# A gated recurrence whose decays are products raised in place instead of exponentials of sums, in a float32 forward pass on one core

## The reference, cut to what matters

```python
def hg_gate(z, lb):                       # lb is 0 in the first block
    k = (1.0 - lb) * sigmoid(-z)
    log_f = log(lb + (1.0 - lb) * sigmoid(z))
    return k, log_f
# S_t = diag(f_t) S_{t-1} + k_t v_t^T,  o_t = S_t^T q_t, by chunks:
    cum = cumsum(lf)
    s_new = exp(last)[..., None] * s + einsum('bhsd,bhse->bhde', kc * exp(last - cum), vc)
    o_inter = einsum('bhtd,bhde->bhte', qc * exp(cum), s)
    decay = exp(where(mask, cum[t] - cum[s], -inf))
    att = einsum('bhtd,bhsd,bhtsd->bhts', qc, kc, decay)
    o = o_inter + einsum('bhts,bhse->bhte', att, vc)
```

## Time and profile before

| | |
|---|---|
| runs | 4153.04, 4154.2, 4158.31 us |
| profiled execution | 4154.1 us, span 4152.8 us, clock 0.941 |
| busy in the span | PE 3831.2 us (92%), DVE 1727.9 (42%), ACT 1230.5 (30%), POOL 216.7 (5%) |
| recurrence, first block | from 437.6 to 592.05 us |
| recurrence, second block | from 1536.2 to 1653.88 us |

### The profile page before, as it was taken

How to read it: one execution, slowest core, us unless ns; L and a number is a source line. 1 busy time by engine, 2 the same in 40 slices (tenths; PEclk the granted TensorE clock), 3 DMA queues, 4 the chain that set the end, 5 groups by cost and what they waited for, 6 DMA issues and landing times.

```text
span 4152.8 us, 46787 instructions
## 1 busy us (share of the span) xinstructions
PE 3831.2 (92%) x20116; PEld 3083.9 (74%) x20116; DVE 1727.9 (42%) x2151; ACT 1230.5 (30%) x1582; POOL 216.7 (5%) x162
## 2 busy tenths in 40 slices
PE   7989678999998876999989989889998999998997
PEld 5866577888887556788868867568886887676886
DVE  3135764222233267433443346543335334354334
ACT  3125432211122263322232234432223223333222
POOL 0000320000000014000000002000000000000000
PEclk9989779999998996999999999899999999999998
DMA  6415101111121100222312222012222222221222
GB/s 247 149 58 188 50 18 47 68 61 61 61 72 61 67 6 1 81 102 93 109 68 95 101 92 81 21 70 92 102 95 78 91 102 101 71 91 62 101 94 79
DMA packets 47709, 341.74 MB, mean 82 GB/s; under 512 B 5280, under 2 KB 5440, under 8 KB 7696
## 3 DMA queue, kind: packets, MB, share of 16 engines
q1 hardware_dynamic: 41184, 301.09, 20.3%
q0 software_dynamic: 5280, 35.57, 2.3%
q10 hardware_dynamic: 1040, 2.10, 0.1%
HBM read 336.63 MB, written 2.10 MB: 82 GB/s over the span
## 4 chain that ended last, share of the span: by engine, by line
PE 86%; DVE 9%; ACT 3%; issue 1%; POOL 1%; DMA 1%; DVEq 0%; ACTq 0%; POOLq 0%
PE PS L349 66%; PE PS L351 7%; PE PS L815 2%; DVE SQ L443 2%; PE PS L831 1%; PE PS L1386 1%; PE PS L870 1%; PE PS L390 1%; PE PS L1112 1%; DVE nmax_a L965 1%; DVE YS L1829 1%; PE PS L409 1%; DVE att L1579 1%; PE PS L502 1%; DVE X L1836 1%
## 5 line engine op out<-in xcount | busy, mean ns | idle before, releaser
L326 DVE TENSOR_TENSOR WL<-raw,WH 128x2048 fp32r<-128x2048 f32 x260 | 595.9, 2292 | 414.9 <-ACT WH L321 414.9
L321 ACT ACTIVATE WH<-raw 128x2048 fp32r<-128x2048 f32 x260 | 495.4, 1905 | 464.5 <-PE PS L349 346.6
L349 PE MATMUL PS<-XH_ff,WH 128*128 128x512 f32 x704 | 280.4, 398 | 12.1 <-DVE XL_ff L454 12.1
L349 PE MATMUL PS<-XH_b,WH 128*128 128x512 f32 x704 | 276.9, 393 | 11.9 <-DVE XL_b L454 10.5
L349 PE MATMUL PS<-XH_a,WH 128*128 128x512 f32 x704 | 277.1, 394 | 11.4 <-DVE XL_a L454 10.0
L349 PE MATMUL PS<-XH_ff,WL 128*128 128x512 f32 x704 | 280.2, 398 | 0.0
L349 PE MATMUL PS<-XL_ff,WH 128*128 128x512 f32 x704 | 277.7, 394 | 0.0
L349 PE MATMUL PS<-XL_a,WH 128*128 128x512 f32 x704 | 275.5, 391 | 0.0
L349 PE MATMUL PS<-XH_a,WL 128*128 128x512 f32 x704 | 275.3, 391 | 0.0
L349 PE MATMUL PS<-XL_b,WH 128*128 128x512 f32 x704 | 275.2, 391 | 0.0
L349 PE MATMUL PS<-XH_b,WL 128*128 128x512 f32 x704 | 275.0, 391 | 0.0
(11 more groups left out here) (356 smaller groups left out, 7815.5 us busy)
## 6 DMA issues: line engine op xcount, KB each, us to landing
raw<-in_panels SPq DMA_DIRECT2D x260, 1024.0 KB, 4.8
ada_at<-in_ada_panels SPq DMA_DIRECT2D x24, 1024.0 KB, 4.8
ada_win<-in_ada_panels POOLq DMA_DIRECT2D x18, 1024.0 KB, 5.1
ada_start<-in_ada_panels POOLq DMA_DIRECT2D x6, 1024.0 KB, 22.5
FX<-in_dft_x POOLq DMA_DIRECT2D x2, 2048.0 KB, 8.0
X<-in_xT SPq DMA_DIRECT2D x1, 3072.0 KB, 11.2
out<-X ACTq DMA_DIRECT2D x1, 2048.0 KB, 6.9
rope<-in_rope POOLq DMA_DIRECT2D x2, 768.0 KB, 10.0
```

What stands on the lines that cost most here:

```text
L321: H.up(ac.activation(WH[s].rearrange("p k n -> p (k n)"), raw[:, s, :], ACT.Copy), n)
L326: L.up(ve.tensor_tensor(WL[s].rearrange("p k n -> p (k n)"), raw[:, s, :], WH[s].bitcast(F32).rearrange("p k n -> p (k n)"), ALU.subtract), n)
L349: t = te.matmul(PS[:, j, :], lhsT, x[:, k, 0:SEQ], start=st, stop=end)
```

## The change

The decays are products of gates rather than exponentials of sums. `tot[d][2h]` holds the product of the gates of each block of 2h tokens, made by multiplying the two halves of `tot[d][h]`. The units run from h = 1 to 64, with the directions alternating (`level_of`). QP (queries times gates) and the keys in U are raised in place: after unit u, the queries of the later halves are multiplied by the product of their earlier half, and the keys of the earlier halves by the product of their later half, which makes them ready for unit u + 2 of the same direction. DVE raises the queries (in the first block those of one of the two feature tiles; POOL those of the other), POOL raises the keys of all 768 tokens. After the last unit QP and the keys are what `state_outputs` and `turn_keys` need. `diffs`, `exps`, the scan, the logarithms, `starts` and the factors on POOL go away.

There is one `att` for both directions. Units 12 and 13 (h = 64) multiply only the 64 early keys and are copied by ACT without a mask. The self products (key sum times query) move to POOL and their matmul behind unit 5; increments and states of both directions come after the last unit; the mask arrives as bytes. Cut to its core:

```diff
-        b["cum"] = shelf.take(f"cum_{l}", [P, 2, 2, TOK])
-        b["ring"] = [shelf.take(f"ring{s}_{l}", [P, 2, TOK]) for s in range(3)]
-        b["att"] = [shelf.take(f"att{d}_{l}", [P, 2, 2 * (NT if l == 0 else NX), P]) for d in range(2)]
+        for k in ("F", "QP"):
+            b[k] = [shelf.take(f"{k}{d}_{l}", [P, 2, TOK]) for d in range(2)]
+        b["KQ"] = shelf.take(f"KQ_{l}", [P, 2, TOK])
+        b["att"] = shelf.take(f"att_{l}", [P, 2, 2 * (NT if l == 0 else NX), P])
+        b["tot"] = [{h: shelf.take(f"tot{d}{h}_{l}", [P, 2, TOK // h]) for h in (2 << i for i in range(LEVELS))}
+                    for d in range(2)]
...
         def level_of(u):
-            return u // LEVELS, u % LEVELS, P >> (u % LEVELS + 1)
+            return u % 2, 1 << (u // 2)
+        def level_bank(u, g, hh):
+            return 4 * (u % 2) + 2 * g + hh
+        def self_bank(l, fc):
+            return 2 * fc if l == 0 else 2 + fc
+        def own_features(l, g):
+            if l == 0:
+                return slice(1, 2) if g else slice(0, 1)
+            return None if g else slice(0, 2)
+        def raise_queries(eng, l, u, f):
+            q = halves(b["QP"][d][:, f, 0:N], h)[:, :, :, late]
+            by = totals(l, d, h)[:, f, 0:N // h].rearrange("p f (b t) -> p f b t", t=2)[:, :, :, d:d + 1]
+            return eng.tensor_tensor(q, q, by.broadcast_to([P, f.stop - f.start, N // (2 * h), h]), ALU.mult)
+        def raise_keys(eng, l, u):
+            k = halves(mix1[l]["U"][:, UFF + 2 * d:UFF + 2 * d + 2, :], h)[:, :, :, early]
+            by = totals(l, d, h).rearrange("p f (b t) -> p f b t", t=2)[:, :, :, 1 - d:2 - d]
+            return eng.tensor_tensor(k, k, by.broadcast_to([P, 2, TOK // (2 * h), h]), ALU.mult)
 # gp_hgrn
+            G.up(gp.tensor_tensor(b["KQ"][:, :, 0:N], U[:, UFF:UFF + 2, 0:N], U[:, UFB:UFB + 2, 0:N], ALU.add))
+            gp.wait_ge(*G.now())
+            G.up(gp.tensor_tensor(b["KQ"][:, :, 0:N], b["KQ"][:, :, 0:N], U[:, UHQ:UHQ + 2, 0:N], ALU.mult),
+                 (name, "kq"))
             for u in range(UNITS):
-                gp.wait_ge(*A[(name, "exp", u)])
-                gp.tensor_tensor(ww[:, :, :, late], ww[:, :, :, late], qq[:, :, :, late], ALU.mult)
-                G.up(gp.tensor_tensor(ww[:, :, :, early], ww[:, :, :, early], kk[:, :, :, early], ALU.mult), ...)
+                gp.wait_ge(*T[(name, "level", u, len(hgrn_groups(l)) - 1)])
+                if u >= 2:
+                    gp.wait_ge(*V[(name, "tot", level_of(u))])
+                    gp.wait_ge(*G[(name, "raised", u - 2)])
+                t = raise_keys(gp, l, u)
+                f = own_features(l, 1)
+                if f:
+                    t = raise_queries(gp, l, u, f)
+                G.up(t, (name, "raised", u))
 # te_hgrn: level(u), after the waits for QP and keys, or for raised u - 2 of G and V
+                            keys = early if h == HD else slice(0, P)
+                            t = te.matmul(PS[keys, to, x * HD:(x + 1) * HD],
+                                          U[r, UFF + 2 * d + f, j * P + keys.start:j * P + keys.stop],
+                                          queries[:, :, late], start=True, stop=True)
+            for g in range(3):
+                turn_values(g)
+            for u in range(UNITS):
+                level(u)
+                if u == 5:
+                    self_products(0)
+                    self_products(1)
+            for d in range(2):
+                turn_keys(d)
+                increments(d)
+            outputs()
+            for d in range(2):
+                state_outputs(d)
 # ac_hgrn, in this order: sigmoids, values, silu, units 12 and 13, turned keys
+                A.up(ac.activation(b["F"][d][:], z, ACT.Sigmoid), (name, "sg", d))
+                A.up(ac.activation(z, z, ACT.Sigmoid, scale=-1.0), (name, "sk", d))
+                A.up(ac.activation(b["hVT"][:, 2 * g:2 * g + 2, :], ...ACT.Copy), (name, "v", g))
+            for u in (UNITS - 2, UNITS - 1):
+                        ac.wait_ge(*V[(name, "pred", UNITS - 3, g, hh)])
+                        A.up(ac.activation(b["att"][early, hh, 2 * c0:2 * c1, late], PS[early, ...], ACT.Copy), ...)
 # ve_hgrn
-                    V.up(ve.tensor_scalar(f, f, 2.0 ** -63, None, ALU.max), (name, "f", d, fc))
+                V.up(ve.tensor_tensor(b["QP"][d][:, :, 0:N], U[:, UHQ:UHQ + 2, 0:N], F[:, :, 0:N], ALU.mult),
+                     (name, "QP", d))
+            for h in (2 ** i for i in range(LEVELS)):
+                for d in range(2):
+                    V.up(ve.tensor_tensor(b["tot"][d][2 * h][:].unsqueeze(3), parts[:, :, :, 0:1], parts[:, :, :, 1:2],
+                                          ALU.mult), (name, "tot", (d, 2 * h)))
+            for u in range(UNITS):
+                raised(u)
+                if u < UNITS - 2:
+                    preds(u)
+                if u == 5:
+                    self_terms(0)
+                    self_terms(1)
+            for d in range(2):
+                states(d)
```

More of the change, by code:

```diff
@@ L1370, in increments, with into @@
[L1370 to L1378, removed]
+                for to in increment_banks(d):
+                    bank(to, V, name, "S", d)
+            opened = set()
+            def into(j, f, hh):
+                to = 4 + 2 * f + j // 4
+                first = (to, hh) not in opened
+                opened.add((to, hh))
+                return PS[hh * HD:(hh + 1) * HD, to, (j % 4) * P:(j % 4 + 1) * P], first
@@ L1379, in level, with outputs @@
+            def outputs():
+                te.wait_ge(*V[(name, "preds")])
+                te.wait_ge(*A[(name, "preds")])
+                for to in range(4, 8):
                     wait_bank(to)
-                    wait_bank(to + 1)
-                    for x in range(2 * (c1 - c0)):
-                        j, f = c0 + x // 2, x % 2
+                for j in range(N // P):
+                    for f in range(2):
                         for hh in range(2):
[L1384 to L1405, removed]
+                            to, first = into(j, f, hh)
@@ L1406, in outputs, with state_outputs @@
+                            te.matmul(to, b["hVT"][:, j, f * P + hh * HD:f * P + (hh + 1) * HD],
+                                      b["att"][:, hh, 2 * j + f, :], start=first, stop=False, skip_group_check=True)
+            def state_outputs(d):
+                te.wait_ge(*V[(name, "S", d)])
+                te.wait_ge(*V[(name, "raised", UNITS - 2 + d)])
                 for j in range(N // P):
-                    i = order.index(j)
+                    i = visits(d).index(j)
                     for f in range(2):
@@ L1445, in ac_hgrn @@
             fence(ac, f"at{l}")
-            for fc in range(2):
-                A.up(ac.activation(U[:, UG + fc, 0:N], U[:, UG + fc, 0:N], ACT.Silu), (name, "g", fc))
             if l:
@@ L1462, in ac_hgrn @@
-            for d in range(2):
-                ac.wait_ge(*V[(name, "end", d)])
-                edge = P - 1 if d == 0 else 0
-                A.up(ac.activation(b["el"][d][:], b["cum"][:, d, :, edge::P], ACT.Exp), (name, "el", d))
-                A.up(ac.activation(b["ring"][d][:], b["ring"][d][:], ACT.Exp), (name, "end", d))
-            def keys(d):
-                if d:
-                    ac.wait_ge(*T[(name, "inc", 0)])
+                z = U[:, UFF + 2 * d:UFF + 2 * d + 2, :]
+                A.up(ac.activation(b["F"][d][:], z, ACT.Sigmoid), (name, "sg", d))
@@ new lines, in ac_hgrn @@
+            for u in (UNITS - 2, UNITS - 1):
+                late, early = sides(*level_of(u))
+                for g, (c0, c1) in enumerate(hgrn_groups(l)):
+                    ac.wait_ge(*T[(name, "level", u, g)])
+                    for hh in range(2):
+                        ac.wait_ge(*V[(name, "pred", UNITS - 3, g, hh)])
+                        A.up(ac.activation(b["att"][early, hh, 2 * c0:2 * c1, late],
+                                           PS[early, level_bank(u, g, hh), 0:2 * (c1 - c0) * HD].rearrange(
+                                               "p (c t) -> p c t", t=HD), ACT.Copy),
+                             (name, "pred", u, g, hh), (name, "preds"))
@@ L1482, in starts @@
-            def starts(d):
-                cu = b["cum"][:, d, :, 0:N]
-                A.up(ac.activation(cu, cu, ACT.Exp), (name, "start", d))
-            keys(0)
-            exps(0)
-            keys(1)
-            for u in range(1, UNITS):
-                exps(u)
-                if u % LEVELS == LEVELS - 1:
-                    starts(u // LEVELS)
             for fc in range(2):
```

280 lines of the change are left out of this document (116 added, 164 removed).

## The result

The changed kernel took 4059.2 us (median of 4 runs, 4054.4 to 4074.3) against 4156.3 for the kernel before beside it: ratio 0.977, 95% interval 0.9741 to 0.9799. Two later series of it gave 0.9815 (0.9789 to 0.9842) and 0.9794 (0.9769 to 0.9819). Forecast were 4097 us and 57 us less; by their ratios the three series say 96, 77 and 86 us less.

What follows compares the result with a forecast made beforehand. DVE bounds the first block's units, PE close behind; afterwards PE bounds. Savings of 35 us in the first block and 22 in the second, together 57 off 4154.1, give 4097 us; range 4076 to 4117.

Steps and rivals of the forecast that it cites:

- Prologue: Ahead of unit 0, log, scan, distances and factors go: unit 0 at 446.3 us instead of 479.25 in the first block.
- The start of the units: Unit 2 waits for DVE's 14 block products and first raise: stall 3.4 us (0 to 6) in the first block.
- Units at 1.2 GHz: Recurrence units in the lower clock: PE bounds at 5.39 us (first block) and 3.6 (second), plus stalls of 2 and 4.
- the rival that had it wait each time: DVE or turn-taking bounds the units: every DVE raise waits for POOL's keys; 4114 us, chance 0.16.
- The clock: Each block has one 9 us stretch of higher clock behind the self products, at 3.5 us a unit (2.5 in the second).
- the bare end: Behind the last unit: turned keys and increments 11.5 us, pairs 2.84, states about 6, no longer hidden in the first block.
- The prediction's own sign of being wrong: Wrong if POOL's products exceed 5 us a unit, PEclk stands at 1.00 in units, or DVE, not PE, never idles there.
- The first rival: Higher clock for all units: some 16 us less in the first block, 9 in the second; 4072 us, chance 0.12.
- h = 64: Units 12 and 13 load only 64 keys: 2.7 us for 48 matmuls and 1.8 for 32, or no gain (5.39).
- POOL's repeated operand: POOL's key raises in the units, never shown with a repeated operand, at plain price; up to twice as upper end.
- The slower rival: POOL's products with a repeated operand far slower: 2.7 times plain price spends the gain, three times gives 4170 us; chance 0.04.

Runs made afterwards that it cites:

- spread products: Changed kernel with DVE's block products spread two by two behind the first units' masked copies, not all ahead of the first raise: 4068.5 us, 0.9789 to the kernel before.
- late self products: Changed kernel with the self products behind unit 11 instead of unit 5: 4091.5 us, ratio 0.9852 to the kernel before.

## Why the prediction was wrong

The range began at 4076 us; the direction and the mechanism were right, the size was not.

- **Prologue.** Right. Unit 0 stood 8.8 us behind ACT's first table load in the first block (449.17 less 440.41), 8.8 forecast; in the second 8.9, forecast 9.1.
- **The start of the units.** Stalls of 7.8 and 10.0 us instead of 3.4 and 4.5. DVE's turns with POOL were foreseen at the upper end (457) and were worse, DVE was through at 464.4: two products took 8.31 us and the rest as long again, because each POOL operation (3.4 and 4.0 us, then 2.9, 1.5, 2.2 and 1.3) held a DVE product until it had ended. That cost 4 and 5 us against the forecast, and the spread products show that it was this queue.
- **Units at 1.2 GHz.** 20.75 us for units 2 to 5 instead of 23.6, 14.0 instead of 18.4 in the second block: the stalls for DVE (2 and 4 us) did not come. DVE starts its raise 0.05 us ahead of POOL's keys and so pays no turn; the rival that had it wait each time failed here, and came true in the kernel with spread products.
- **The clock. This is the step that failed.** "I give each block one such stretch of 9 us": in the first it lasted from 492 to past 530 us. Units 6 to 13 took 21.5 us instead of 33.5, and the bare end 15 instead of 20.5, since it too ran at 2.4 GHz. That is 12 + 5 us of the first block's 16 beyond the forecast (51 against 35; the rest of the terms cancel). In the second block the forecast's 9 us were near (7 us in two profiles, none in the third), and only the end was faster, 13.3 us instead of 18. The prediction's own sign of being wrong, PEclk at 1.00 in the units, came true from unit 6 on. The 9 us came from a stretch of the kernel before which ended at 496.6 us, when PE had just stood idle for 3.2; I took it for the length that such a stretch has, and let it only be shorter in the range. The same trace has a second fast stretch, of 13.7 us (547.8 to 561.4), that also ended behind a wait. PE behind the two waits (kernel before):

```profile
496.18 5.07 PE L1386 MATMUL PS<-ring 64*128 64x64 f32 x48 [3.20 <-DVE att L1579]
...
560.53 4.60 PE L1386 MATMUL PS<-ring 64*128 64x64 f32 x48 [2.67 <-DVE att L1579]
```

In the changed kernel PE's gaps in the fast stretch are 0.2 us, and 1.06 ahead of the last unit. The self products' share (moving them costs 13.4 us) is shown by a run; that a wait loses the clock is only likely (it fell behind those of 0.96, 2.67, 3.14 and 3.20 us in the blocks and behind that of 4.0 to 4.2 us between them, and not behind those of 1.06 and 1.60 us ahead of the last unit).

- The first rival, the fast clock for all units, had the wrong cause and part of the effect: 8 of 14 units were fast in the first block, three or none in the second. By the Trainium skill ("TensorE: Matmul & The Clock Gate", the table of the two states) sustained activity suffices. For these matmuls 31.00 of 31 us busy at 0.50 in the kernel with late self products, and 45.78 us without a gap at 0.51 in another, go against it.
- **h = 64.** Forecast as 5.4 and 3.7 us of gain. In the first block nothing, since at the fast clock POOL's 2.7 us set the distance; in the second 2.9 in the units, and 2.2 behind them by a clock that came back later.
- **POOL's repeated operand.** Plain price: 1.95 us a raise of 768 elements, 0.88 for 384 (means of units 2 to 13). The slower rival is out.
- **Readings.** In the stretch of the earlier trace rows the units of the kernel before stood 7.3 us apart (496.18 to 539.73 for six), not 6.7, and 22.9 us over 28 copies are 0.82 each, not the 0.885 taken. No term of the sum hangs on either.
- **What is no part of it:** 10.8 us of the first profile's gain lie in the feed-forward stage and come and go with the run. From the blocks alone the gain is 76 to 81 us, that is 4073 to 4078 us, at the lower end of the range (4076) and 19 to 24 below the 4097. So how far below the range the first series fell is in part luck; that the first block gained 51 us instead of 35 is not, since three profiles agree within 0.1 us.

What stays open: what makes the clock fall in the second block, where no wait above 0.42 us stood ahead of the fall in the changed kernel. The share of time that PE works does not decide alone. It was 3.58 of 4 us there before the fall, and 18.25 of 21 in the first block with spread products, where it held; in the second block units of 32 matmuls fell and units of 48 held in every profile. And why the feed-forward stage has two rates, and the attention two lengths, was not tried.

## What to carry to other kernels

Before a change that removes waits, ask at which clock TensorE will stand afterwards, and don't read the length of a fast stretch from a trace in which a wait ended it: here the clock made 17 us of difference to the forecast. What brings it up (here full-width matmuls) belongs as early as it costs nothing, and with no long wait behind it: where 3 us followed, the clock fell and the block was 14 us longer. Where two engines take turns, as DVE and POOL do here with products of two SBUF operands, the one that comes 0.1 us late waits for the other's instruction (1.91 us instead of 0.56), so keep small work from standing just ahead of the one on the path. And measure a gain of 1% by the length of the stage that was changed, when the rest of the run has lengths of its own that come and go by 10 us.

## What the runs showed of the hardware

- Matmuls with 128 stationary and 64 moving columns over 64 rows, without a gap on PE, stood at 1.2 GHz for 51.5 us (self products behind unit 11); eight rows of full-width matmuls (4.9 us) ahead of them put them at 2.4 GHz to the end of the recurrence's matmuls, in all three profiles of the changed kernel.
- Doing half more matmuls made units faster: 2.7 us for 48 of them at 2.4 GHz against 3.4 for 32 at 1.2 (second block; 17.84 less 1.61 over six units, 22.65 less 1.97 over six).
- The same program, with TensorE granted its full clock and never idle, ran the feed-forward stage in 555.5 us in one profile and 565.9 in another. Over all fourteen profiles it lay at 555.5 to 556.9 us or at 565.9 to 567.3, never between.
- Behind the same wait of PE of 4.0 to 4.2 us the granted clock fell in all fourteen profiles; in eleven it was back within 4 us, in three after 24 us.
- A DVE product of 128x384 with both operands in SBUF took 0.56 us when it started just ahead of POOL's product and 1.26 to 1.91 us when it started behind; one of 128x768 took 4.2 us beside a POOL operation of 3.4 or 4.0 us.
